# The latent's second recurrence: outputs laid with tokens first, a column of ones beside the values, and keys times queries computed once per head

## What is computed

```python
def mlstm_chunk_scan(q, k, v, ig, logf, state0):
    def step(carry, xs):
        C, n, m = carry
        ...
        D = jnp.where(mask, bh[..., :, None] - bh[..., None, :] + igh[..., None, :], -jnp.inf)
        m_inter = bh + m[..., None]
        m_t = jnp.maximum(D.max(-1), m_inter)
        S = jnp.einsum('bthd,bshd->bhts', qc, kc) * jnp.exp(D - m_t[..., None])
        w_inter = jnp.exp(m_inter - m_t)
        num = (jnp.einsum('bhts,bshe->bthe', S, vc)
               + jnp.swapaxes(w_inter, 1, 2)[..., None] * jnp.einsum('bthd,bhde->bthe', qc, C))
        den = S.sum(-1) + w_inter * jnp.einsum('bthd,bhd->bht', qc, n)
        h = num / jnp.swapaxes(jnp.maximum(jnp.abs(den), jnp.exp(-m_t)), 1, 2)[..., None]
        ...
        C_new = decay[..., None, None] * C + jnp.einsum('bhs,bshd,bshe->bhde', wk, kc, vc)
        n_new = decay[..., None] * n + jnp.einsum('bhs,bshd->bhd', wk, kc)
        return (C_new, n_new, m_new), h
    ...
def bidirectional_prefix(scan_fn, ctx_dirs, lat_dirs, state0):
    ...
    return outs_c[0] + outs_c[1], outs_l[0] + outs_l[1]
```

## Time and profile before

| | us |
|---|---|
| median of 3 runs | 3534.76 |
| lowest and highest | 3530.82, 3542.27 |
| the profiled execution | 3537.52 |
| its span on the core | 3535.7 |
| granted TensorE clock, mean | 0.93 of full speed |

### The profile page before, as it was taken

One profiled execution on the slowest core, in us unless ns is written; L12 is line 12 of the kernel. 1 busy time (PEld: TensorE's weight loads), 2 busy tenths in 40 slices (PEclk: granted clock), 3 DMA queues, 4 the chain that ended last, 5 costly groups with the idle time before them and its releaser, 6 DMA issues.

```text
span 3535.7 us, 41174 instructions
## 1 busy us (share of the span) xinstructions
PE 3224.5 (91%) x16508; PEld 2657.7 (75%) x16508; DVE 1866.8 (53%) x3026; ACT 1125.2 (32%) x1537; POOL 1149.3 (33%) x296
## 2 busy tenths in 40 slices
PE   5888999988888999997998989879999898979996
PEld 4645888866378788786888989768888776768885
DVE  3753778847645563764507754449665427341113
ACT  3342222123434432324326543232123324332221
POOL 2202334422036333323434443023434220124441
PEclk8898999988999999998999988679999789979998
DMA  6202445522034322223333332125553220113331
GB/s 112 66 13 65 127 144 180 171 68 66 13 93 142 96 81 87 72 72 107 107 90 108 108 96 72 60 72 166 168 172 114 69 70 1 29 53 98 96 95 48
DMA packets 481710, 324.36 MB, mean 92 GB/s; under 512 B 103616, under 2 KB 448832, under 8 KB 481008
## 3 DMA queue, kind: packets, MB, share of 16 engines
q1 hardware_dynamic: 477056, 310.37, 29.9%
q10 hardware_dynamic: 2656, 6.30, 0.5%
q0 software_dynamic: 1808, 5.05, 0.5%
HBM read 316.41 MB, written 5.24 MB: 91 GB/s over the span
## 4 chain that ended last, share of the span: by engine, by line
PE 77%; DVE 13%; ACT 4%; issue 2%; SPq 2%; POOL 1%; DMA 1%; DVEq 0%; ACTq 0%
PE G L2459 11%; PE G L2468 10%; PE G L2469 10%; PE G L2473 10%; PE G L2628 5%; PE G L2629 5%; PE G L2633 5%; PE G L2483 3%; PE M L2510 2%; PE M L2808 2%; DVE rstd L1389 1%; POOL WL L663 1%; ACT WH L714 1%; PE S L2459 1%; SPq L544 1%
## 5 line engine op out<-in xcount | busy, mean ns | idle before, releaser
L663 POOL TENSOR_TENSOR WL<-raw,WH 128x2048 fp32r<-128x2048 f32 (+1 forms) x260 | 1132.5, 4357 | 2200.3 <-ACT WH L714 2200.3
L714 ACT ACTIVATE WH<-raw 128x2048 fp32r<-128x2048 f32 (+1 forms) x260 | 468.1, 1801 | 685.3 <-PE G L2633 417.8
L2468 PE MATMUL G<-hH,WH 128*128 128x512 f32 x1520 | 595.6, 392 | 0.0
L2469 PE MATMUL G<-hL,WH 128*128 128x512 f32 x1520 | 592.8, 390 | 0.0
L2473 PE MATMUL G<-hH,WL 128*128 128x512 f32 x1520 | 360.1, 389 | 0.0
L2468 PEld LDWEIGHTS G<-hH,WH 128*128 128x128 f32 x1520 | 285.9, 188 | 60.1
L2469 PEld LDWEIGHTS G<-hL,WH 128*128 128x128 f32 x1520 | 286.0, 188 | 59.0
L2473 PEld LDWEIGHTS G<-hH,WL 128*128 128x128 f32 x1520 | 285.3, 188 | 59.2
L1452 DVE SCALAR_TENSOR_TENSOR acc<-adaw,cvec,acc 128x512 f32<-128x512 f32 x280 | 289.1, 1086 | 4.2
L2459 PE MATMUL G<-hH,WH 128*128 128x512 f32 (+1 forms) x448 | 172.8, 386 | 16.0 <-POOL WL L663 13.4
L2459 PE MATMUL G<-hL,WH 128*128 128x512 f32 (+1 forms) x448 | 171.3, 382 | 0.0
(11 more groups left out here) (657 smaller groups left out, 6413.3 us busy)
## 6 DMA issues: line engine op xcount, KB each, us to landing
raw<-ffn_w_in_in SPq DMA_DIRECT2D x264, 256.0 KB, 4.0
adaw<-ada_w_in SPq DMA_DIRECT2D x48, 1024.0 KB, 5.3
raw<-ab_w_in_in SPq DMA_DIRECT2D x128, 256.0 KB, 3.5
raw<-ffn_w_out_in SPq DMA_DIRECT2D x96, 256.0 KB, 3.5
raw<-w_gate_in SPq DMA_DIRECT2D x88, 256.0 KB, 3.4
raw<-w_up_in SPq DMA_DIRECT2D x88, 256.0 KB, 4.4
raw<-w_down_in SPq DMA_DIRECT2D x64, 256.0 KB, 3.4
raw<-w_in_in SPq DMA_DIRECT2D x40, 256.0 KB, 3.8
```

The lines of the kernel that those rows point to most:

```text
L663: nc.gpsimd.tensor_tensor(WL[c % 2][:, 0:size_of[c]], raw[c % 2][:, 0:size_of[c]], WH[c % 2][:, 0:size_of[c]].bitcast(F32), ALU.subtract)\
L714: nc.scalar.activation(WH[c % 2][:, 0:cols], raw[c % 2][:, 0:cols], ACT.Copy).then_inc(weights_hi, 1)
L2468: mm(dst, view(WH[c % 2], k), high, start=(k == 0 and not (joint and i)), stop=False)
L2469: mm(dst, view(WH[c % 2], k), low, start=False, stop=False)
```

## The change

The outputs of the second recurrence are computed with tokens on the partitions. `st` and `qw`, which were the moving operands, become the stationary ones; the moving operands are the values with a column of ones beside them (`vb` is laid out as 4 heads of 132 columns, and column 128 is set to one once) and the state with its column of key sums (`cs`, 129 columns, as before). So a matmul of 129 columns gives outputs and denominator together, and the same holds for `pairs_b`. The denominators lie on the same partitions as the outputs, so DVE applies the reciprocal as a per-partition factor: for d = 0 into a new tile `ways` ("both" in the trace), for d = 1 multiplied and added to it. For d = 1 alone, PE turns the two 128 x 128 tiles back into `S[1]` (`turned_b`), and DVE copies them to `ob`. The products of keys and queries are made in units with d = 0 only, each half in its own half of `G[3]`, and read by both directions.

```diff
@@ Latent.__init__
-                    f("vb", N // P, 4 * P), f("qb", 2, N), f("kb", 2, N), f("bg", N))
+                    f("vb", N // P, HA, P + 4), f("qb", 2, N), f("kb", 2, N), f("bg", N))
...
-                    f("cs0", 2, P + 4), f("cs1", 2, P + 4), f("dcol", 2, 2))
+                    f("cs0", 2, P + 4), f("cs1", 2, P + 4), f("dcol", 2, 2), f("both", 2, N // P, P))
@@ DVE, latent_columns
-                        own(V.tensor_copy(dst[:, k, 256 * j:256 * j + 256], G[g % 4][:, 0:256]), f"{name}{g}")
+                        if name == "bv":
+                            own(V.tensor_copy(dst[:, k, 2 * j:2 * j + 2, 0:P], G[g % 4][:, 0:256].rearrange("p (h v) -> p h v", h=2)), f"{name}{g}")
...
+                own(V.memset(ps.vb[:, :, :, P:P + 4], 1.0), "bv.one")
@@ DVE, latent_recurrence: sums_b
-                    own(V.scalar_tensor_tensor(dcol, S[1][:, o:o + 2], -1.0, em2, ALU.mult, ALU.max), f"B{u}.low")
...
-                    own(V.tensor_tensor(dcol, dcol, S[1][:, o:o + 2], ALU.max), f"B{u}.low2")
+                    own(V.scalar_tensor_tensor(dcol, bank[:, :, P], -1.0, ps.colE[:, 2 * half:2 * half + 2, 32 * d + h], ALU.mult, ALU.max), f"B{u}.low")
+                    dve.wait_ge(dve_done, here())
+                    own(V.tensor_tensor(dcol, dcol, bank[:, :, P], ALU.max), f"B{u}.low2")
                     dve.wait_ge(dve_done, here())
                     own(V.reciprocal(dcol, dcol), f"B{u}.inv")
+                    dve.wait_ge(dve_done, here())
+                    for q in range(2):
+                        way = ways[:, 2 * half + q, :]
+                        if d:
+                            own(V.scalar_tensor_tensor(way, bank[:, q, 0:P], dcol[:, q:q + 1], way, ALU.mult, ALU.add), f"B{u}.way")
+                        else:
+                            own(V.tensor_scalar(way, bank[:, q, 0:P], dcol[:, q:q + 1], None, ALU.mult), f"B{u}.way")
@@ DVE: out_b
-                    if d == 0:
-                        own(V.tensor_copy(low, bank[:, TC:2 * TC]), f"B{u}.by")
...
-                        own(V.tensor_tensor(ps.ob[:, h, cut], bank[:, 0:TC], low, ALU.mult), f"B{u}.o")
-                    else:
-                        own(V.tensor_copy(low, bank[:, TC:2 * TC]), f"B{u}.by")
...
-                        own(V.tensor_tensor(low, bank[:, 0:TC], low, ALU.mult), f"B{u}.oo")
...
-                        own(V.tensor_tensor(ps.ob[:, h, cut], ps.ob[:, h, cut], low, ALU.add), f"B{u}.o")
+                    if d:
+                        dve.wait_ge(pe_done, at("pe", f"t.B{u}.turned"))
+                        own(V.tensor_copy(ps.ob[:, h, cut], S[1][:, p * TC:p * TC + TC]), f"B{u}.o")
@@ DVE: kept_b
-                    own(V.tensor_tensor(st_of(u), x_of(u), G[3][:, 0:TC], ALU.mult), f"B{u}.st")
+                    own(V.tensor_tensor(st_of(u), x_of(u), G[3][:, unit(u)[4]], ALU.mult), f"B{u}.st")
@@ PE: rows_b
-                    for q in range(2):
-                        o = half * TC + q * P
-                        last = mm(G[3][:, q * P:q * P + P], ps.kb[rows, h // 2, o:o + P], ps.qb[rows, h // 2, o:o + P], start=True, stop=True)
+                    if d == 0:
+                        for o in (half * TC, half * TC + P):
+                            last = mm(G[3][:, o:o + P], ps.kb[rows, h // 2, o:o + P], ps.qb[rows, h // 2, o:o + P], start=True, stop=True)
@@ PE: pairs_b
-                        mm(S[0][rows, q * TC:q * TC + P], ps.kw[:, q, :], ps.vb[:, 2 * half + q, h * P:h * P + P], start=True, stop=True)
-                        last = mm(S[0][rows, q * TC + P:q * TC + P + 1], ps.kw[:, q, :], ones[:, 0:1], start=True, stop=True)
+                        last = mm(S[0][rows, q * TC:q * TC + P + 1], ps.kw[:, q, :], ps.vb[:, 2 * half + q, h, 0:P + 1], start=True, stop=True)
@@ PE: out_b
-                    if u:
-                        pe.wait_ge(dve_done, at("dve", f"t.B{u - 1}.low2"))
                     if u >= 2:
-                        pe.wait_ge(dve_done, at("dve", f"t.B{u - 2}.o"))
+                        pe.wait_ge(dve_done, at("dve", f"t.B{u - 2}.way"))
...
-                        mm(M[u % 2][:, cut], ps.vb[:, 2 * half + q, h * P:h * P + P], st[:, cut], start=True, stop=False)
-                        mm(M[u % 2][:, cut], cs[rows, t, 0:P], qw[rows, cut], start=False, stop=True)
-                        mm(S[1][:, col], st[:, cut], ones[:, 0:1], start=True, stop=False)
-                        last = mm(S[1][:, col], qw[rows, cut], cs[rows, t, P:P + 1], start=False, stop=True)
+                        cut, dst = slice(q * P, q * P + P), M[u % 2][:, q * TC:q * TC + P + 1]
+                        mm(dst, st[:, cut], ps.vb[:, 2 * half + q, h, 0:P + 1], start=True, stop=False)
+                        last = mm(dst, qw[rows, cut], cs[rows, t, 0:P + 1], start=False, stop=True)
@@ PE: shares_b becomes turned_b
-                        last = mm(M[u % 2][:, TC + q * P:TC + q * P + P], ps.dcol[:, u % 2, q:q + 1].broadcast_to([P, P]), ident[:, :], start=True, stop=True)
...
+                    if d == 0:
+                        return
+                    pe.wait_ge(dve_done, at("dve", f"t.B{u}.way"))
+                    if u >= 3:
+                        before = u - 1 if p else u - 3
+                        pe.wait_ge(dve_done, at("dve", f"t.B{before}.o"))
+                    for q in range(2):
+                        o = p * TC + q * P
+                        last = nc.tensor.transpose(S[1][:, o:o + P], ps.ways[:, h % 2, 2 * half + q, :], ident[:, :])
...
-                        shares_b(s - 3)
+                        turned_b(s - 3)
```

More of the change, by code:

```diff
@@ L2054, in tokens @@
                         dve.wait_ge(pe_done, at("pe", f"t.{name}{g}"))
-                        own(V.tensor_copy(dst[:, k, 256 * j:256 * j + 256], G[g % 4][:, 0:256]), f"{name}{g}")
+                        if name == "bv":
+                            own(V.tensor_copy(dst[:, k, 2 * j:2 * j + 2, 0:P], G[g % 4][:, 0:256].rearrange("p (h v) -> p h v", h=2)), f"{name}{g}")
+                        else:
+                            own(V.tensor_copy(dst[:, k, 256 * j:256 * j + 256], G[g % 4][:, 0:256]), f"{name}{g}")
                 added_sums("c.y1", TC)
@@ L2286, in sums_b @@
                     h, d, p, half, _ = unit(u)
-                    o, dcol = 2 * (u % 2), ps.dcol[:, u % 2, :]
-                    em2 = ps.colE[:, 2 * half:2 * half + 2, 32 * d + h]
+                    bank, dcol, ways = M[u % 2][:, :].rearrange("p (q c) -> p q c", q=2), ps.dcol[:, u % 2, :], ps.ways[:, h % 2, :, :]
                     dve.wait_ge(pe_done, at("pe", f"t.B{u}.o"))
-                    own(V.scalar_tensor_tensor(dcol, S[1][:, o:o + 2], -1.0, em2, ALU.mult, ALU.max), f"B{u}.low")
@@ L2296, in out_b @@
+                    for q in range(2):
+                        way = ways[:, 2 * half + q, :]
+                        if d:
+                            own(V.scalar_tensor_tensor(way, bank[:, q, 0:P], dcol[:, q:q + 1], way, ALU.mult, ALU.add), f"B{u}.way")
+                        else:
+                            own(V.tensor_scalar(way, bank[:, q, 0:P], dcol[:, q:q + 1], None, ALU.mult), f"B{u}.way")
                 def out_b(u):
                     h, d, p, half, cut = unit(u)
-                    bank, low = M[u % 2], rstd[:, 0:TC]
@@ L3187, in rows_b @@
                     mm(G[2][:, 0:TC], to_rows, ps.both[0][:, cut], start=True, stop=True)
-                    mm(G[2][:, TC:2 * TC], to_rows, ps.both[1][:, cut], start=True, stop=True)
-                    for q in range(2):
-                        o = half * TC + q * P
-                        last = mm(G[3][:, q * P:q * P + P], ps.kb[rows, h // 2, o:o + P], ps.qb[rows, h // 2, o:o + P], start=True, stop=True)
+                    last = mm(G[2][:, TC:2 * TC], to_rows, ps.both[1][:, cut], start=True, stop=True)
+                    if d == 0:
+                        for o in (half * TC, half * TC + P):
+                            last = mm(G[3][:, o:o + P], ps.kb[rows, h // 2, o:o + P], ps.qb[rows, h // 2, o:o + P], start=True, stop=True)
                     last.then_inc(pe_done, did("pe", f"t.B{u}.rows"))
@@ L3228, in shares_b, with turned_b @@
+                def turned_b(u):
+                    h, d, p, half, _ = unit(u)
+                    if d == 0:
[4 more added lines that the diff above has]
+                        pe.wait_ge(dve_done, at("dve", f"t.B{before}.o"))
                     for q in range(2):
-                        last = mm(M[u % 2][:, TC + q * P:TC + q * P + P], ps.dcol[:, u % 2, q:q + 1].broadcast_to([P, P]), ident[:, :], start=True, stop=True)
@@ L3230, in shares_b @@
-                    last.then_inc(pe_done, did("pe", f"t.B{u}.bc"))
+                        o = p * TC + q * P
+                        last = nc.tensor.transpose(S[1][:, o:o + P], ps.ways[:, h % 2, 2 * half + q, :], ident[:, :])
+                    last.then_inc(pe_done, did("pe", f"t.B{u}.turned"))
                 for s in range(UNITS + 3):
```

10 lines of the change are left out of this document (1 added, 9 removed).

## The result

The changed kernel took 3485.4 us (median of 4 runs, 3480.7 to 3489.0) beside 3536.9 us for the kernel before (4 runs, 3530.8 to 3542.3): a ratio of 0.9851, with a 95% interval from 0.9836 to 0.9865. It is faster by 1.5%. The forecast was 3470, its range 3455 to 3494. The time is inside the range, in its slower half, and 15 us from the forecast. The profiled execution took 3485.9 us, its span 3484.1.

The account below looks back on a forecast made before the run. PE alone was taken to bound the covered stretch, and a DVE-PE chain the uncovered end. Gains of 48.3 and 17 us made 65 off 3537.5, giving 3472, or 3470 us from the median; range 3455 to 3494.

Parts of the forecast that it names:

- items 1 to 4: PE's covered steps, full clock: `out_b` saves 16.1 us, `pairs_b` 3.6, transposes for `shares_b` 3.8, keys times queries 4.9.
- the 111.2 of the sum: Covered stretch: its 141.1 us of full-clock time less the 29.9 us saved leaves 111.2 us.
- The rival that it does not recover: Covered stretch: slow spells come after each step as before; covered gain 35.6 us, kernel 3485 us; chance 0.22.
- 8.5 us allowed: Covered stretch: 7 us for the first slow spell after the gates' wait, 1.5 for spells among down-product pieces.
- The concern about transposes: Covered stretch: new PE transposes do not count as work for the clock gate, which would leave a 35.6 us gain.
- PE's waits (item 5): Covered stretch: `out_b` waits for an earlier DVE scaling instead of the output, saving 1.5 of 1.9 us of PE idle.
- What costs nothing: DVE loses two or three 0.42 us operations a step, gets 0.58 or 1.13, and stays under half of the stretch.
- The chain at the low clock, 18.8 us: Uncovered end: the DVE and PE chain after the change, 7.0 plus 11.8 us; 13.6 at the full clock.
- The choice of 16: Uncovered end: 16 us taken between 13.6 at the full clock and 18.8 at the low, a gain of 17.
- The third, a new chain in PE's place: Gate and up pieces: `st` waits for ACT, giving back 14 to 28 us, kernel 3484 to 3498; chance 0.06.
- a kernel slower than before: Covered stretch: PE's clock falls for good; at 0.50 it takes 222 us and the kernel 3575; chance 0.03.
- 48.3 + 17: Gains forecast for the covered stretch, 48.3 us, and the uncovered end, 17 us, together 65 us.

Follow-up runs that it names:

- no_copy: The changed kernel with the key weighting moved from DVE to ACT and the copy of the carried state removed: 3472.3 us, ratio 0.9816.
- onecol_keys_back: The changed kernel with key weighting on ACT, four unread one-column matmuls per unit put back, and keys times queries in all 16 units: 3513.3 us, ratio 0.9933.

## Why the prediction was nearly right, and what it missed

- **The bound.** Right: the covered stretch is PE's, and work taken from it came off the time. The matmuls cost what items 1 to 4 said; pairs 0.56 against 0.5, transposes 0.19 against 0.3, `out_b` 1.67 against 1.66. From 2068 to 2190.7, the stretch of the new kernel that matches 2065 to 2233 of the old, work and idle time at the full clock were 122.7 x 0.95 = 116.6 us against the 111.2 of the sum. PE's idle time explains 3.7 of that difference, the rest is near the rounding of the clock (0.01 is 1.2 us).
- **The clock.** Right: it recovered, from 0.84 to 0.95, at 1.00 for 80 us on end. The rival that it does not recover gave the very time that was measured, 3485, and is false: had it been true, the covered gain would have been 35.6, and it was 45.4. A time alone would have chosen the wrong rival. The spells were over-sized: 8.5 us allowed, and 122.7 x 0.05 = 6.1 lost; in no_copy 115.4 x 0.02 = 2.3. This error went against the one of the bound, so the covered gain is near the forecast in part by luck. The concern about transposes fell away: no_copy and the change have twelve of them in the stretch, and no_copy's clock is 1.00 from 2078 to 2183 with all of them in it. What the Trainium skill says of them ("TensorE: Matmul & The Clock Gate", Part 4: PE-mode transpose) cost nothing here.
- **PE's waits (item 5).** Wrong, in sign. I took off 1.5 of 1.9 us of idle time; it rose to 4.1. The wait of `out_b` for the output did go; the new idle time is the pairs' wait for DVE's states. The step that failed is the paragraph "What costs nothing": it took DVE's busy time for cover and put it under half of the stretch. Its own numbers did not give that, since 73.3 us of the 119.7 forecast are 0.61. And DVE was busy for 94.4 of 125.7 us, because an instruction that POOL holds counts as busy; in no_copy it is 55.9 of 115.4.
- **The end.** The chain at the low clock, 18.8 us, was nearly right (its check is below). The choice of 16 was wrong. It rested on a drop of the clock only some 8 us into the end of the kernel before, and that was misread: the earlier trace rows has 0.50 for all of that end, and in the earlier trace rows its first pairs already take 0.66 us where the earlier trace rows has 0.43. In the new kernel too the clock was low after the first long wait:

```profile
2189.89 4.51 POOL L663 TENSOR_TENSOR WL<-raw,WH 128x2048 fp32r<-128x2048 f32 x1 [9.74 <-ACT WH L714]
...
2190.70 0.42 DVE L2259 TENSOR_TENSOR ht<-G,hide 128x256 f32<-128x256 f32 x1 [0.63 <-PE G L3189]
...
2191.69 2.92 DVE L2272 TENSOR_SCALAR t_kw<-t_ktb,t_colW 128x64 f32<-128x64 f32 x2
...
2195.48 1.09 PE L3203 MATMUL S<-t_vb,t_kw 128*64 128x129 f32 x4 [4.82 <-DVE t_cs L2285]
2196.50 0.80 PE L3217 MATMUL M<-t_vb,ht 128*128 128x129 f32 x2
```

  `out_b` takes 0.80 where it took 0.49 in step 13. And the key weighting of the last covered unit, held until POOL's instruction ended at 2194.40, added 2.5 us to the chain: 18.8 + 2.5 = 21.3, against 22.0 from DVE's first instruction to its last. Of the 5.9 us that the end fell short, this hold is about 2.5 and the clock 2.8. In no_copy the whole end is 18.6 us, but with 0.65 us of key weighting and copy taken out of it in each of two steps.
- **The rivals.** The third, a new chain in PE's place, is what happened in kind, but on DVE, and with an instruction that the change did not touch. I had the row for it, and used it only to say that a kernel slower than before "would need ten such hits without cover". That was true, but a few such hits take back part of a gain, and the sum had no term for them. The new scaling, which I named as the one that could be hit, never was.
- **The sum.** 48.3 + 17 became 45.4 + 11.1; 2.9 more went to the start of the section and 2.0 to the heads, both inside what profiles of unchanged code scatter. With the holds gone, no_copy measured 3472, but not term by term: covered 52.7, end 15.4, start of the section -3.0, against 48.3, 17 and 0. That its time is 2 us from the forecast is in part luck.
- **The signs.** Of those that the prediction named, the step (3.47 us), the clock (0.95) and the stretch (122.7) came true. PE was busy for 97% of the stretch and not 98%, its idle time stayed under the 5 us at which the bound would have been wrong, and the end was 22.8 and not 16.

**What stays open.** What makes the clock fall behind a hold. The two profiled executions of the change and of no_copy are 13.6 us apart: 7.3 in the covered stretch, 4.2 in the end and 2.1 in the heads. The 7.3 are PE's idle time (4.1) and the second slow spell (6.8 us at half the clock, 3.4), within rounding. That the spell follows from the idle time is argued from their order; both go when the holds go, and no run here has one without the other. Why onecol_keys_back kept its clock. Whether the start of the gates' stage has a cause other than scatter. And whether a slower POOL instruction, or POOL's work cut in smaller pieces, would do as well as taking DVE's work away; it was not tried.

## What to carry to other kernels

Before you count an engine's busy time as cover, ask which of its short instructions take far longer than their shape: that time can be a wait, and it turns dear as soon as another engine stops hiding it. Such a hold goes to the next instruction of the same kind when you move only one away; take away all of them in the step, or none. And check the mechanism, not only the time: here a wrong rival had the right number.

## What the runs showed of the hardware

Which DVE instructions POOL holds was plain in the new trace (ns, least/median/most, first and last start):

```profile
L1452 DVE SCALAR_TENSOR_TENSOR acc<-adaw,cvec,acc x280: 734/741/5041, 368.2 to 2622.4; 128x512 f32<-128x512 f32 x140
...
L2102 DVE TENSOR_TENSOR c_FL<-c_silu,c_FH x22: 424/425/4837, 1865.0 to 2158.9; 128x256 fp32r<-128x256 f32 x22
...
L2176 DVE SCALAR_TENSOR_TENSOR t_states<-t_states,t_steps,S x56: 346/348/349, 1895.9 to 2027.2; 128x128 f32<-128x128 f32 x56
...
L2285 DVE SCALAR_TENSOR_TENSOR t_cs<-t_cs,dec,S x16: 342/350/358, 2089.0 to 2204.8; 64x129 f32<-64x129 f32 x16
```

Some forms whose tensors all lie in SBUF (the first two, and the key weighting and the copy) stretch to the end of POOL's 4.6 us. Not all do: of the reciprocals of `ncol` (L1396), nine started while POOL's instruction was in work and took 166 to 178 ns, as the others did, and the eight fills of `sq` (L1817) took 272 ns each. Those that read a tensor from PSUM (S, M or G) never do: 46 of the 56 of L2176 started while POOL's instruction was in work, and the slowest took 349 ns. The Trainium skill ("SBUF — State Buffer", Who interferes with whom) calls it an exclusive lock on a port pair that the second to start waits for in full; the trace agrees, and adds that a copy of 0.22 us can wait 3 us for it.
